# Sums of squares of the attention output as two single-pass products of split squares, with one quarter-tile of matmuls placed behind the last attention

## The reference, cut to what matters

```python
def rms_norm(x, g):
    xf = x.astype(jnp.float32)
    y = xf * lax.rsqrt(jnp.mean(jnp.square(xf), axis=-1, keepdims=True) + RMS_EPS)
    return y * g.astype(jnp.float32)

    # in hybrid_mixer
    o = gla_chunked(q, k, v, log_a)                 # [B, S, 4, 128]
    o = rms_norm(o, gla_norm_g).astype(h.dtype)
    y_gla = (o * jax.nn.silu(g.reshape(B, S, GLA_HEADS, GLA_DV))).reshape(B, S, GLA_WIDTH)
```

## Time and profile before

| what | value |
|---|---|
| median of 3 runs | 2130.92 us (2130.78 to 2133.38) |
| the profiled execution: its time | 2129.42 us |
| the profiled execution: span | 2127.7 us |
| TensorE busy | 2066.7 us, 97% |
| VectorE busy | 1388.0 us, 65% |
| ScalarE busy | 995.4 us, 47% |
| GpSimd busy | 508.6 us, 24% |
| TensorE clock granted | 0.995 of full |

### The profile page before, as it was taken

The page is one execution under the profiler, slowest core; times in us unless marked ns, Lnnn a source line. Parts: engine busy times, 40 slices in busy tenths (PEclk is TensorE's granted clock), DMA queues, the critical chain, the costliest instruction groups (busy, mean ns, idle before and its releaser), DMA issues.

```text
span 2127.7 us, 28928 instructions
## 1 busy us (share of the span) xinstructions
PE 2066.7 (97%) x11384; PEld 1684.6 (79%) x11384; DVE 1388.0 (65%) x1929; ACT 995.4 (47%) x1339; POOL 508.6 (24%) x479
## 2 busy tenths in 40 slices
PE   6999999999999999999999999999999999999998
PEld 5777787778777877787888788888788888778877
DVE  4668566756765678765565775665675645964577
ACT  4525354445445445655455654544433333633333
POOL 4001010202010213111100254444694700720000
PEclk9999999999999999999999999999999999999999
DMA  6222334323332523356546778678968666676564
GB/s 201 60 60 78 116 85 130 108 83 126 101 118 61 168 71 125 126 184 229 192 166 240 251 266 283 240 272 281 330 218 281 201 190 196 213 230 190 197 208 159
DMA packets 241767, 374.33 MB, mean 176 GB/s; under 512 B 16496, under 2 KB 117968, under 8 KB 241632
## 3 DMA queue, kind: packets, MB, share of 16 engines
q1 hardware_dynamic: 212672, 272.68, 39.8%
q0 software_dynamic: 28960, 99.81, 13.6%
HBM read 272.81 MB, written 99.61 MB: 175 GB/s over the span
## 4 chain that ended last, share of the span: by engine, by line
PE 53%; DVE 5%; DMA 2%; ACT 2%; issue 1%; POOL 0%; SPq 0%; DVEq 0%; ACTq 0%
PE main L68 9%; PE main L70 9%; PE main L69 9%; PE sc L68 6%; PE sc L70 6%; PE sc L69 6%; DVE w_lo L1620 2%; PE aux L70 1%; PE ob L69 1%; PE ob L70 1%; PE aux L69 1%; PE ob L68 1%; PE aux L68 1%; DMA x_piece<-normed_dram 1%; DMA w_b<-in_w_ff_dram 1%
## 5 line engine op out<-in xcount | busy, mean ns | idle before, releaser
L1620 DVE TENSOR_TENSOR w_lo<-w_b,w_hi 128x1024 fp32r<-128x1024 f32 x142 | 207.7, 1465 | 221.4 <-ACT w_hi L1587 221.0
L1620 DVE TENSOR_TENSOR w_lo<-raw,w_hi 128x1024 fp32r<-128x1024 f32 x142 | 197.5, 1394 | 120.8 <-ACT w_hi L1587 120.6
L1587 ACT ACTIVATE w_hi<-raw 128x1024 fp32r<-128x1024 f32 x142 | 150.1, 1059 | 233.2 <-PE main L70 96.3
L1587 ACT ACTIVATE w_hi<-w_b 128x1024 fp32r<-128x1024 f32 x142 | 150.0, 1057 | 163.1 <-PE aux L70 73.4
L1063 DVE TENSOR_TENSOR w_lo<-raw,w_hi 128x1024 fp32r<-128x1024 f32 x116 | 141.2, 1223 | 120.8 <-ACT w_hi L767 120.1
L68 PE MATMUL main<-xT_lo,w_hi 128*128 128x512 f32 (+1 forms) x528 | 216.2, 410 | 1.5 <-DVE xT_lo L1075 1.5
L70 PE MATMUL main<-xT_hi,w_hi 128*128 128x512 f32 (+1 forms) x528 | 205.6, 389 | 0.0
L69 PE MATMUL main<-xT_hi,w_lo 128*128 128x512 f32 (+1 forms) x528 | 205.4, 389 | 0.0
L68 PE MATMUL sc<-x_lo,w_hi 128*128 128x512 f32 x448 | 174.9, 390 | 2.6 <-DVE z L2082 2.1
L767 ACT ACTIVATE w_hi<-raw 128x1024 fp32r<-128x1024 f32 x116 | 122.3, 1055 | 116.7 <-DMA raw<-in_w_in_dram 53.5
L68 PE MATMUL main<-x_lo,w_hi 128*128 128x512 f32 x448 | 174.8, 390 | 2.0 <-ACT z L1961 1.9
(11 more groups left out here) (282 smaller groups left out, 4735.4 us busy)
## 6 DMA issues: line engine op xcount, KB each, us to landing
raw<-in_w_in_dram SPq DMA_DIRECT2D x80, 512.0 KB, 3.9
h_dram<-z SPq DMA_DIRECT2D x64, 512.0 KB, 3.9
raw<-h_dram SPq DMA_DIRECT2D x112, 256.0 KB, 2.7
w_b<-h_dram SPq DMA_DIRECT2D x112, 256.0 KB, 2.7
h_dram<-h_s SPq DMA_DIRECT2D x48, 512.0 KB, 3.2
rows<-in_x_dram POOLq DMA_DIRECT2D x32, 512.0 KB, 5.1
raw<-in_w_out_dram SPq DMA_DIRECT2D x32, 512.0 KB, 3.7
raw<-in_w_ff_dram SPq DMA_DIRECT2D x32, 512.0 KB, 6.4
```

The source lines that it names most:

```text
L1587: act.activation(hi, slot_tile(ff, m), ACT.Copy).then_inc(ff.hi_done, 1)
L1620: dve.tensor_tensor(lo, slot_tile(ff, m), hi.bitcast(F32), ALU.subtract).then_inc(ff.lo_done, 1)
```

## The change

The squares are split as the weights are: `sq_hi`, a rounded fp32r copy by ScalarE, and `sq_lo`, the rest, by VectorE; `mean_square` multiplies ones (read as fp32r) by both, in two single-pass matmuls that add up in the same bank. ScalarE waits for its two squares before it copies them. The two tensors lie in the places of `xqT` and of part of `xp` and `xpT`, which are free then. VectorE makes `sq_lo` at the end of pair 0 behind the split for B0, and at the end of pair 1 ahead of the split for B1. TensorE's `mean_square` now waits for `sq_lo`. And one quarter leaves the five between the two `mean_square` of pair 0 and comes behind the last `attend` of pair 1.

```diff
-ACT_STEPS_FIRST, ACT_STEPS = 12, 24
+ACT_STEPS_FIRST, ACT_STEPS = 16, 28
...
+        with ExitStack() as at_xqT:
+            sq_hi = at_xqT.enter_context(nc.sbuf_tensor("sq_hi", [P, 2, BLK], F32R))
         xqT = sb("xqT", [P, 2, BLK])
...
+        with ExitStack() as at_xp:
+            sq_lo = at_xp.enter_context(nc.sbuf_tensor("sq_lo", [P, 2, 2, BLK], F32R))[:, :, 1, :]
         xp = sb("xp", [P, 4, M])
...
+        sq_hi_done = sem("sq_hi_done")
...
                 pe.wait_ge(sq_ready, 4 * t + 2 * hp + e + 1)
-                pe.matmul(aux[:, :], ones[:, :], rr[:, e, :], start=True, stop=True).then_inc(aux_done, 1)
+                every = ones[:, :].bitcast(F32R)
+                pe.matmul(aux[:, :], every, sq_lo[:, e, :], start=True, stop=False)
+                pe.matmul(aux[:, :], every, sq_hi[:, e, :], start=False, stop=True).then_inc(aux_done, 1)
...
                 mean_square(t, 0, 0)
-                quarters(5)
+                quarters(4)
                 mean_square(t, 0, 1)
                 quarters(1)
...
                     attend(t, 1, c)
-                quarters(1)
+                quarters(2)
                 mean_square(t, 1, 0)
                 quarters(1)
                 mean_square(t, 1, 1)
...
-            def square(t, hp):
+            def square(t, hp, steps):
                 act.wait_ge(on_ready, 4 * t + 2 * hp)
                 act.wait_ge(ob_free, OB_USES * t + OB_GLA + 4 * hp + 4)
                 for e in range(2):
-                    act.activation(rr[:, e, :], oT[:, e, :], ACT.Square).then_inc(sq_ready, 1)
+                    steps.mark(act.activation(rr[:, e, :], oT[:, e, :], ACT.Square))
+                steps.settle()
+                for e in range(2):
+                    act.activation(sq_hi[:, e, :], rr[:, e, :], ACT.Copy).then_inc(sq_hi_done, 1)
...
+            def square_low(t, hp):
+                for e in range(2):
+                    dve.wait_ge(sq_hi_done, 4 * t + 2 * hp + e + 1)
+                    dve.tensor_tensor(sq_lo[:, e, :], rr[:, e, :], sq_hi[:, e, :].bitcast(F32), ALU.subtract
+                                      ).then_inc(sq_ready, 1)
...
                 update_state(t, 0, 3)
                 next_split(t, J_B0)
+                square_low(t, 0)
                 decayed(t, 1)
...
                 update_state(t, 1, 3)
+                square_low(t, 1)
                 next_split(t, J_B1)
```

More of the change, by code:

```diff
@@ L963, in mixer_block @@
                 copy_o(t, 0, 3)
-                square(t, 0)
+                square(t, 0, steps)
                 exponentials_k(t, 1)
@@ L984, in mixer_block @@
                 copy_o(t, 1, 3)
-                square(t, 1)
+                square(t, 1, steps)
                 inverse_rms(t, 1, 0)
```

## The result

The changed kernel takes 2142.07 us (median of 6 executions, 2140.56 to 2144.49) against 2130.85 for the kernel before beside it (6 executions, 2127.99 to 2133.38): a ratio of 1.0052, 95% interval 1.0041 to 1.0062, or 11.2 us slower. The forecast was 2137.1 with a range to 2141.0: the sign was right, the size too small. The profiled execution took 2142.4 us with a span of 2140.4, 12.7 us more than before, at a mean granted clock of 0.991 against 0.995. Of all the executions behind the numbers of this document one is left out of its ratio: one of the eight of e9 took 3436.75 us at a mean granted clock of 0.557 (the median of the other seven is 2120.63 us).

What follows compares the result with a forecast made beforehand. TensorE, busy 97% of the span, was taken as the bound, with VectorE setting the pace at pair 1's chunk 1. Per block, +0.70 and the lock's 0.84 gave 1.54; 4 x 1.54 = 6.2 us: 2137.1 us, range 2131.5 to 2141.

Steps and rivals of the forecast that it cites:

- The products: TensorE's sums of squares: two single passes replace an fp32 product, saving 0.40 us each, 16 x 0.40 = 6.4 us.
- Rival D: Two-product form saves less, each pass taking 0.39 us: +9 us, 2140 us; chance 0.02.
- The split and the first wait: Pair 0's end: ScalarE's copies and VectorE's low parts delay the first sum, TensorE idling 2.19 us instead of 0.32.
- What stands behind the wait: Pair 0 after the first sum's wait: products and four quarters (5.46 us) keep pace, pair 1's scores starting 0.31 us earlier.
- The lock: Pair 1's first masks: GpSimd's y_lo blocks VectorE on shared ports, chain 0.53 us later, price 0.84 us a block.
- Pair 1: From attend of chunk 1: one quarter more, 0.6 us idle ahead of its first sum, second sum's end +0.70 us.
- The sum: Whole kernel: 1.54 us a block, four blocks, 6.2 us slower, 2137.1 us from the median.
- A: No collision of GpSimd with pair 1's masks: +0.70 us a block, 2.8 us in all, 2133.7 us; chance 0.20.
- B: New waits hidden, mainly at pair 0's first sum, only products count: 6.4 us less, 2124.5 us; chance 0.08.
- C: Weight for C1 lands late, delaying attend of chunk 0: +8 to +10 us, 2140 us; chance 0.12.
- The sign: Whole kernel: slower by over 0.2% (over 2135.2 us), given 0.67; same 0.24, faster 0.09.

Runs made afterwards that it cites:

- e9: Kernel before, squares written in fp32r by ScalarE and summed in one pass, low part left out: 2121.7 us (before 2131.43), ratio 0.9956.
- e2: Kernel before, fp32 product replaced by two single passes over squares rounded to fp32r, low part left out, no split: 2124.87 us (before 2130.66), ratio 0.9974.
- e1: The changed kernel run again as it is: 2139.04 us (before 2130.66), ratio 1.0041.
- e5: Kernel before with only the quarter moved, from between pair 0's sums to ahead of pair 1's first: 2135.5 us (before 2130.89), ratio 1.0016.
- e7: Kernel before with only a wait of TensorE for ScalarE's exponentials ahead of pair 0's first sum: 2146.0 us (before 2130.89), ratio 1.0073.
- e3: Changed kernel, with VectorE making pair 0's low parts ahead of the split for B0: 2135.97 us (before 2130.66), ratio 1.0029.
- e8: e3 with ScalarE's y_part 2, and GpSimd's y_lo behind it, moved ahead of the exponentials of pair 1's queries: 2139.75 us, ratio 1.0042.
- e11: e3 with ScalarE's y_part 2 moved ahead of the sigmoid of gate tile 0: 2140.26 us (before 2132.66), ratio 1.0040.
- e10: Changed kernel, ScalarE squaring the output twice (fp32r, fp32) without copies, low parts ahead of the split, y_part as in e8, quarters spread anew: 2133.49 us, ratio 1.0012.

## Why the prediction was right or wrong

**The products: right.** Taken at 0.40 us each, 6.4 in all; e2 measures 5.8 [3.4, 7.7], and 1.50 to 1.58 us a block in its profile. Rival D falls.

**The split and the first wait: right.** Copies and low parts went at the paces taken; these are the rows of ScalarE and VectorE after:

```profile
157.54 1.15 ACT L859 ACTIVATE sq_hi<-rr 128x512 fp32r<-128x512 f32 x2
...
159.26 1.28 DVE L1176 TENSOR_TENSOR sq_lo<-rr,sq_hi 128x512 fp32r<-128x512 f32 x2
```

`sq_lo` at 159.26 + 1.85 = 161.11 (161.14 reckoned), the sum at 161.95 (161.89), 2.25 us idle (2.19).

**What stands behind the wait: the step that failed.** "Then, with 0.34 + 0.23 us for the two products after a wait, four quarters (5.46)" took the pace of 0.227 for granted on either side of a 2.2 us hole. The quarters took 1.6 us more in three blocks of four, and those blocks 0.9 us more in all than the fourth. None of the rows that I used spoke of it, yet the trace of before has one: in block 3 TensorE idles 4.04 us, waiting for `v_rows`, and the table by stretches of before shows the clock behind that:

```profile
748.00:750.00 2.00, 1.07 (x8) 1.10 (x8) 1.23 (x1) 2.00 (x5) 0.00 (x0) 0.89 0.22 56
750.00:752.00 2.00, 2.00 (x46) 1.45 (x49) 0.78 (x1) 1.47 (x3) 0.00 (x0) 0.50 0.60 144
```

All its other idle times in the attention are at most 1.3 us. Outside the attention the trace of before has nearer rows: five idle times of 1.86 to 2.69 us after the first 50 us, with a fall behind two (1.91 us at 69.01, 1.90 at 2069.61) and none behind three (1.86 at 890.44, 2.69 at 966.43, 2.08 at 1193.49). So a chance of about a half could have been read for a wait of 2.2 us, and the sum has no term for it.

**The lock: right where it could be seen.** In block 3, where the clock held, the masks take 1.22 us, 0.73 more than the 0.49 of before (the price was put at 0.84), and `attend` of chunk 1 is 0.51 later (0.53 forecast). In the other blocks the slow clock put the scores behind GpSimd's turn, which ended at 170.14 + 1.85 = 171.99, as reckoned (172.01). The two delays overlap, so the clock costs 1.38 - 0.51 = 0.87 us a block and not 1.6; and the idle time at that `attend` is 1.28 there, not 2.1. Where the clock held it is nearly the forecast's: 1.98 us in block 0 of e1, and in block 3 of the change 0.59 at chunk 0 and 1.17 at chunk 1.

**Pair 1: right.** Idle 0.45 ahead of its sum (0.6), +0.95 to +0.99 from chunk 1 to the next block (1.54 - 0.53 = 1.01), the wait at the next block 1.00 as before.

**The sum.** 6.2 us forecast; 4 x 1.46 = 5.8 by block 3's measure; 8.5 with three falls. e1's 8.4 is near that partly by chance: its own four stretches add up to 9.2, and its start is earlier too. That the first measurement gave 11.2 lies at parts that belong to no edit, which the two profiles show at 3.4 us (`v_rows`) and 2.7 (behind the mixer), less 1.85 at the start. "Nothing behind the mixer touches the change" holds, but that stretch scatters by more than the whole forecast. Whether the change makes the short form of `y_lo` more frequent wasn't settled; it also occurs in kernels without a split (e9, and most blocks of e2, e5 and e7).

**The rivals.** A (no collision) and B (hidden) didn't occur. C, a late weight, gave a time of 2140, which is near, and its chain occurred: in block 3 of the change, and of e1, the copy of the keys comes late and `attend` of chunk 0 waits 0.59 and 0.77 us for it. But it cost nothing there, as that stretch is no longer than forecast; the nearness of its time is luck. The upper end, 2141.0, was C's half; a rival "the hole slows what follows" at three blocks times 1.6 us would, by an estimate from the rows of after, have put the range to 2142 and the likeliest at about 2140. That rival was not on record; it is read off afterwards.

**The sign: right, for the reason given.** The change loses because the split's chain, ScalarE's two copies and VectorE's split and subtraction, stands on the path at pair 0's end and costs more than the products give.

## What to carry to other kernels

A wait that a change adds to TensorE is priced in two parts: its length, and the pace of what follows. Where the trace has idle times of that length, look at the granted clock behind them first, in the whole trace and not only near the change; here waits of 1.2 us that stand alone were never followed by a fall, and waits of 2.25 us were in about half the cases. Cutting such a wait to half was worth its falls (0.8 us a block) and nothing more, because another engine's queue set the pace behind it. To tell a fall from the rest, compare the same stretch block by block within one execution, which scatters by 0.1 us where the whole kernel scatters by over 10. And an instruction of GpSimd's that meets VectorE wasn't moved for nothing in a full VectorE queue in any of the kernels here: look for where VectorE idles (before had 1.66 us for it), not for where the victim is.

## What was not expected of the hardware

- The same idle time of 2.25 to 2.27 us was followed by 1.2 GHz in one block and not in another of one execution; matmuls of 128x512 then start 0.427 us apart instead of 0.227, eight of them, for 1.6 us in all.
- One GpSimd subtraction (1.3 us alone) held VectorE in each place that it was moved to: 0.92 us on the masks of pair 1 (e3), 1.10 on the scalings of pair 0 (e8), 1.05 on the masks of chunk 3 (e11). The Trainium skill, page "SBUF — State Buffer", section "SBUF: two separate sides", calls the shared ports an exclusive lock, held for the whole instruction; the three rows agree in that VectorE stands for most of the 1.3 us. It cost nothing where VectorE was idle anyway (before: 1.66 us idle, masks 0.49).
- GpSimd's record seems to start at the asking for its turn, not at the getting: one and the same instruction shows 1.30 us where it is let in at once (e8, e11) and 2.75 where VectorE runs two splits back to back.
- ScalarE's Square writes fp32r at the price of one that writes fp32 (1.16 us for two of 128x512 in e9, as before), so a high part needs no copy behind the square (e9, e10).
